# Expert rows loaded behind block 20, and the last three blocks' tokens computed again in slot order

## The reference

```python
h = rmsnorm(x, g_ffn)
g = top1(softmax(h @ w_group))            # one of 4 groups
e_val, e_top = top2(h @ w_er, group g)    # two of its 8 experts
gate = softmax(e_val) * p_top
x = x + sum_j gate[j] * (silu(h @ w_gate[e_j]) * (h @ w_up[e_j])) @ w_down[e_j]
y = rmsnorm(x, g_final)
```

## Time and profile before

| | |
|---|---|
| median of 3 runs | 1202.7 us (1200.88 to 1203.57) |
| the profiled execution's own time | 1198.68 us |
| its span, first to last instruction | 1196.8 us |
| expert blocks, first gathered row to last row out of PSUM | 856.7 to 1149.6 us |
| from there to the end of the span | 47.2 us |

### The profile page before, as it was taken

One profiled execution on the slowest core, in us unless ns is written; L12 is line 12 of the kernel. 1 busy time (PEld: TensorE's weight loads), 2 busy tenths in 40 slices (PEclk: granted clock), 3 DMA queues, 4 the chain that ended last, 5 costly groups with the idle time before them and its releaser, 6 DMA issues.

```text
span 1196.8 us, 19783 instructions
## 1 busy us (share of the span) xinstructions
PE 1097.5 (92%) x7553; PEld 779.2 (65%) x7553; DVE 613.8 (51%) x1631; ACT 480.7 (40%) x1036; POOL 176.5 (15%) x268
## 2 busy tenths in 40 slices
PE   5997799999999899999999899998499999999946
PEld 4984478787878798888989678787243333333312
DVE  6528978888888786723333472365421212121116
ACT  6437678787878524343343451321011111111113
POOL 1320023434342300000000000000102111111002
PEclk8999999999999999999999999999599999999978
DMA  8343140403111134232532635003889999999748
GB/s 285 50 87 64 35 102 1 114 2 84 32 51 40 34 102 123 80 99 62 142 97 80 215 106 220 38 36 129 338 320 393 419 418 418 418 420 417 291 162 340
DMA packets 127253, 205.46 MB, mean 172 GB/s; under 512 B 15108, under 2 KB 100388, under 8 KB 114868
## 3 DMA queue, kind: packets, MB, share of 16 engines
q1 hardware_dynamic: 114868, 177.63, 42.1%
q0 software_dynamic: 10560, 21.02, 5.2%
q10 hardware_dynamic: 1728, 5.51, 1.2%
HBM read 177.85 MB, written 30.18 MB: 174 GB/s over the span
## 4 chain that ended last, share of the span: by engine, by line
PE 76%; DVE 11%; ACT 4%; DMA 4%; issue 3%; POOL 1%; SPq 0%; DVEq 0%; ACTq 0%; POOLq 0%
PE psum L2498 14%; PE psum L2513 7%; PE psum L2213 5%; PE psum L2215 5%; PE psum L2214 5%; DVE place L1464 3%; PE psum L2185 2%; PE psum L2187 2%; PE psum L2186 2%; PE psum L2295 2%; PE psum L2465 2%; PE psum L2364 2%; PE psum L2366 2%; PE psum L2365 2%; PE psum L2269 2%
## 5 line engine op out<-in xcount | busy, mean ns | idle before, releaser
L2498 PE MATMUL psum<-place,place 128*32 128x512 f32 x1536 | 171.1, 597 | 1.2 <-issue 1.2
L1116 ACT ACTIVATE place<-place,place 128x768 uint8<-128x768 f32 (+3 forms) x128 | 125.6, 984 | 6.8 <-DVE place L1495 6.8
L2213 PE MATMUL psum<-place,place 128*128 128x512 f32 x288 | 121.9, 423 | 2.3 <-DVE place L1452 2.3
L2498 PEld LDWEIGHTS psum<-place,place 128*32 128x32 f32 x1536 | 49.0, 110 | 104.8 <-issue 102.3
L2215 PE MATMUL psum<-place,place 128*128 128x512 f32 x288 | 113.4, 394 | 0.0
L2214 PE MATMUL psum<-place,place 128*128 128x512 f32 x288 | 112.6, 391 | 0.0
L1910 DVE TENSOR_TENSOR place<-psum,place 128x256 f32<-128x256 f32 x24 | 10.2, 425 | 156.3 <-ACT place L1296 156.3
L2513 PE MATMUL psum<-place,place 128*32 128x512 f32 x768 | 86.9, 592 | 0.7 <-DVE place L1904 0.7
L2185 PE MATMUL psum<-place,place 128*128 128x256 f32 x288 | 84.9, 295 | 1.6 <-ACT place L1138 1.6
L2186 PE MATMUL psum<-place,place 128*128 128x256 f32 x288 | 81.4, 283 | 0.0
L2187 PE MATMUL psum<-place,place 128*128 128x256 f32 x288 | 81.4, 283 | 0.0
(11 more groups left out here) (323 smaller groups left out, 2428.3 us busy)
## 6 DMA issues: line engine op xcount, KB each, us to landing
place<-in_w_gate SPq DMA_DIRECT2D x32, 1024.0 KB
place<-in_w_up SPq DMA_DIRECT2D x32, 1024.0 KB
place<-in_w_down SPq DMA_DIRECT2D x32, 1024.0 KB
place<-in_w_in SPq DMA_DIRECT2D x28, 512.0 KB, 6.5
place<-expert_out SPq DMA_DIRECT2D x9, 1024.0 KB, 13.0
place<-in_cache_attn_k SPq DMA_DIRECT2D x32, 256.0 KB, 3.3
place<-in_cache_attn_v SPq DMA_DIRECT2D x32, 256.0 KB, 3.4
place<-in_x_prompt SPq DMA_DIRECT2D x3, 1536.0 KB, 8.6
```

The costliest lines, as they stand in the source:

```text
L1116: last = nc.scalar.activation(reached[j], score[j], ACT.Sign, bias=pivot.bitcast(F32)[:, j:j + 1], scale=-1.0, accum_out=minus[:, j - BY_A ...
L2213: nc.tensor.matmul(bank(4 + b), hT_hi[:, k, rows], hi, start=k == 0, stop=False)
L2498: last = nc.tensor.matmul(bank(b % 2)[rows], xT[b % 2][:, k, rows], w_gu[expert_of(b, q) % NSLOT][:, :, k, :], start=k == 0, stop=k == KD - 1)
```

## The change

1. **Loading behind block 20.** SP no longer waits for all 24 blocks. After the scatters of blocks 0 to 20 it loads all nine `y_in` tiles into weight slots that have come free. Blocks 21 to 23 are scattered into a second tensor, `late_rows_out`, and rows of `expert_out` that belong to them stay zero. Both tensors (9.4 MB each) are filled with zeros by SP during the retention heads 0 and 1.
2. **Late blocks in slot order.** For each of the three late blocks POOL gathers the residual rows of its slots (`late_frames`, from a DRAM copy of `x1` that SP now writes before each normed tile), a small table with gates and the other pick's block (`picks_of`, 12 bytes a row) and the row of the other pick (`other_picks`, once from `expert_out`, once from `late_rows_out`). DVE computes the indices (`late_index_all`, 13 small instructions), adds the block's own rows straight from SBUF (`own_pick`) and the others' (`other_pick`). These three are tiles 9 to 11. They are squared, scaled, and scattered by POOL over `y_p` after all eight prompt tiles are stored.
3. **The sample tile** (8) is summed on PE after the late gathers. `ON_PE` is now (5, 6, 7, 8). The final norm runs over 12 tiles instead of 9, in the order `LAST` = 0, 1, 2, 3, 4, 5, 6, 7, 9, 10, 11, 8.
4. **DVE sums some tiles early.** Tiles 0 and 1 stand before `hidden(23)`, tile 2 (behind `late_index_all`) before `rows_out(22)`, tile 3 before `rows_out(23)`.
5. **Overflow.** The overflow blocks and the tables for them move ahead of block 0, inside an `if 0 < n_over` on each engine. All five engines now read `n_over` there, after a short `over_count` on DVE. `over_frames` on PE runs only inside that branch. The loops at the end are gone.

```diff
-ON_PE, LAST_ORDER = (1, 3, 5, 7), (0, 2, 1, 4, 3, 6, 5, 7, 8)
+CUT = NMAIN - 3
+LATE_BLOCKS = range(CUT, NMAIN)
+NLATE = len(LATE_BLOCKS)
+ON_PE = (5, 6, 7, TP)
+BEFORE_HIDDEN, BEFORE_ROWS, BEFORE_LAST = (0, 1), (2,), (3,)
+EARLY_SQUARES = 2
+ON_DVE = tuple(t for t in range(T) if t not in ON_PE)
 STEPS = RH * T
...
+        y_in = [place(at, 2 * D, "p (j d) -> p j d", j=2) for at in (
+            up_at[2], up_at[2] + 2 * D, dn_at[2], up_at[3], up_at[3] + 2 * D, dn_at[3], up_at[4], up_at[4] + 2 * D, dn_at[4])]
+        other_rows = [place(up_at[1] + D * n, D) for n in range(NLATE)]
...
+        LAST = list(ON_DVE) + list(ON_PE[:-1]) + [T + n for n in range(NLATE)] + [TP]
...
+                if h < 2:
+                    sp.wait_ge(pool_set, 4)
+                    empty = late_rows_out if h else expert_out
+                    sp.dma_start(empty.rearrange("(n p) d -> p n d", p=P), zeros.unsqueeze(1).broadcast_to([P, 2 * T, D])).then_inc(zeroed[0], 16)
...
                 sp.wait_ge(h2_done, t + 1)
+                sp.dma_start(x1_dram[t * P:(t + 1) * P, :], x1[:, t, :]).then_inc(x1_out, 16)
                 sp.dma_start(h2_dram[t * P:(t + 1) * P, :], h2[t % 2]).then_inc(h2_out[t % 2], 16)
...
+            sp.wait_ge(*counted)
+            n_over = sp.value_load(over_meta[0:1, NOVER:NOVER + 1], min_val=0, max_val=NOVER)
+            with sp.If(0 < n_over):
...
-            sp.wait_ge(y_out[0], 16 * NMAIN // 2)
-            sp.wait_ge(y_out[1], 16 * NMAIN // 2)
+            sp.wait_ge(y_out[0], 16 * ((CUT + 1) // 2))
+            sp.wait_ge(y_out[1], 16 * (CUT // 2))
             for t in range(T):
+                if t == 3:
+                    sp.wait_ge(gu_ps, last_block(28) + 1)
+                if t == 5:
+                    sp.wait_ge(dn_ps, last_block(28) + 1)
+                if t == 6:
+                    sp.wait_ge(gu_ps, last_block(29) + 1)
+                if t == TP:
+                    sp.wait_ge(dn_ps, last_block(29) + 1)
                 sp.dma_start(y_in[t], expert_out.rearrange("(j t p) d -> t p j d", j=2, p=P)[t]).then_inc(y_loaded(t)[0], 16)
...
+            def late_frames(n):
+                b = CUT + n
+                if n == 2:
+                    pool.wait_ge(h2tr_ps, T + NMAIN)
+                pool.indirect_dma_start(late_x1[n], None, x1_dram, bass.IndirectOffsetOnAxis(ap=block_frames[:, b:b + 1], axis=0),
+                                        bounds_check=NTOK - 1, oob_is_err=False).then_inc(late_x1_in[0], 16)
...
+                pool.indirect_dma_start(late_picks[:, n, :], None, pick_table, bass.IndirectOffsetOnAxis(ap=block_rows[:, b:b + 1], axis=0),
+                                        bounds_check=2 * NTOK - 1, oob_is_err=False).then_inc(late_picks_in[0], 16)
...
+            def other_picks(n, late):
+                pool.indirect_dma_start(other_rows[n], None, late_rows_out if late else expert_out,
+                                        bass.IndirectOffsetOnAxis(ap=late_others[:, late, n:n + 1], axis=0),
+                                        bounds_check=2 * NTOK - 1, oob_is_err=False).then_inc(others_in[0], 16)
...
+            for b in range(2, NMAIN + 5):
+                if b < NMAIN:
+                    gather(b)
+                if b == NMAIN:
+                    pool.wait_ge(*picks_out)
+                    pool.wait_ge(*late_cleared)
+                    pool.wait_ge(x1_out, 16 * RH + 16 * T)
+                    for n in range(NLATE):
+                        picks_of(n)
+                    late_frames(0)
+                    late_frames(1)
+                if b == NMAIN + 3:
+                    for n in range(2, NLATE):
+                        late_frames(n)
+                    pool.wait_ge(*others_ready)
+                    pool.wait_ge(gu_ps, NMAIN)
+                    pool.wait_ge(y_out[0], 16 * ((CUT + 1) // 2))
+                    pool.wait_ge(y_out[1], 16 * (CUT // 2))
+                    for n in range(NLATE):
+                        other_picks(n, 0)
...
+            for x in range(T + NLATE):
+                root(x)
+                if x == 2:
+                    for m in range(2):
+                        pool.wait_ge(y_out[m], 16 * (NMAIN // 2))
+                    pool.wait_ge(others_in[0], 48 + 16 * NLATE)
+                    pool.wait_ge(*y_loaded(TP))
+                    for j in range(2):
+                        pool.indirect_dma_start(y_in[TP][:, j, :], None, late_rows_out, bass.IndirectOffsetOnAxis(ap=sample_late[:, j:j + 1], axis=0),
+                                                bounds_check=2 * NTOK - 1, oob_is_err=False).then_inc(others_in[0], 16)
+                if 2 <= x < 2 + NLATE:
+                    other_picks(x - 2, 1)
+            for m in range(3):
+                pool.wait_ge(y7_out[m], 16 * ((TP + 2 - m) // 3))
+            y_p = o_["y_p"].rearrange("a s d -> (a s) d")
+            for n in range(NLATE):
+                pool.wait_ge(out_done, TP + n + 1)
+                pool.indirect_dma_start(y_p, bass.IndirectOffsetOnAxis(ap=late_write[:, n:n + 1], axis=0), out_rows[T + n], None,
+                                        bounds_check=SEQ - 1, oob_is_err=False).then_inc(late_out[0], 16)
+            pool.wait_ge(*late_out)
...
+            def square(x):
+                t = LAST[x]
+                if t in ON_PE:
+                    act.wait_ge(wo_ps, T + ON_PE.index(t) + 1)
+                    rows = bank(2 * ON_PE.index(t), 0, D)
+                else:
+                    act.wait_ge(*summed(t))
+                    rows = x1[:, t, :] if t < T else late_x1[t - T]
+                if x:
+                    act.wait_ge(ssq_done, 2 * T + x)
...
+            act.wait_ge(gu_ps, NMAIN)
+            for x in range(EARLY_SQUARES):
+                square(x)
             rows_out(NMAIN - 1)
...
+            for x in range(EARLY_SQUARES, T + NLATE + 3):
+                if x < T + NLATE:
+                    square(x)
+                if x >= 3 and LAST[x - 3] < T:
+                    store(x - 3)
...
+            def over_count():
                 L(v, tt(e_cnt, bank(5, 0, NE), C("base"), ALU.subtract))
                 L(v, tt(t_thr, e_cnt.unsqueeze(2).broadcast_to([P, NE, 9]), C("thr").unsqueeze(1).broadcast_to([P, NE, 9]), ALU.is_gt))
                 L(v, nc.vector.reduce_sum(e_blk, t_thr, AX))
                 L(v, nc.vector.tensor_tensor_scan(e_incl, e_blk, e_blk, 0.0, ALU.add, ALU.max))
+                nc.vector.tensor_copy(over_meta[:, NOVER:NOVER + 1], e_incl[:, NE - 1:NE]).then_inc(slots_done, 1)
+                v.wait_ge(*counted)
...
+            def late_index_all():
+                v.wait_ge(*late_picks_in)
+                L(v, ts(late_absent, late_picks[:, :, 2], float(CUT), 2.0 * NTOK, ALU.is_ge, ALU.mult))
+                L(v, tt(late_others[:, 0], late_rows, late_absent, ALU.add))
+                L(v, ts(late_rows, late_rows, 2.0 * NTOK, None, ALU.add))
+                L(v, tt(late_others[:, 1], late_rows, late_absent, ALU.subtract))
+                for n in range(NLATE):
+                    L(v, ts(late_absent[:, n:n + 1], late_picks[:, n, 2:3], float(CUT + n), None, ALU.is_equal))
+                    L(v, ts(late_rows[:, n:n + 1], late_picks[:, n, 2:3], float(CUT + n), 8.0 * NTOK, ALU.is_gt, ALU.mult))
+                L(v, tt(late_second, late_second, late_absent, ALU.mult))
+                L(v, nc.vector.scalar_tensor_tensor(late_frame, late_second, -4.0, late_frame, ALU.mult, ALU.add))
+                tt(late_write, late_frame, late_rows, ALU.add).then_inc(others_ready[0], 1)
...
+            def early_sum(t):
+                v.wait_ge(*y_loaded(t))
+                L(v, nc.vector.scalar_tensor_tensor(x1[:, t, :], y_in[t][:, 0, :], gates[:, 0, t:t + 1], x1[:, t, :], ALU.mult, ALU.add))
+                nc.vector.scalar_tensor_tensor(x1[:, t, :], y_in[t][:, 1, :], gates[:, 1, t:t + 1], x1[:, t, :], ALU.mult, ALU.add).then_inc(x2_done, 1)
+            def own_pick(n):
+                if n == 0:
+                    v.wait_ge(*late_x1_in)
+                    v.wait_ge(y_act, NMAIN)
+                    v.wait_ge(y_dve, NMAIN)
+                nc.vector.scalar_tensor_tensor(late_x1[n], y_of(CUT + n), late_picks[:, n, 0:1], late_x1[n], ALU.mult, ALU.add).then_inc(own_done[0], 1)
+            def other_pick(n):
+                if n == 0:
+                    v.wait_ge(*others_in)
+                v.wait_ge(own_done[0], own_done[1] + n + 1)
+                nc.vector.scalar_tensor_tensor(late_x1[n], other_rows[n], late_picks[:, n, 1:2], late_x1[n], ALU.mult, ALU.add).then_inc(x2_done, 1)
...
+                if b + 1 == NMAIN:
+                    for t in BEFORE_HIDDEN:
+                        early_sum(t)
                 hidden(b)
+                if b + 1 == NMAIN:
+                    late_index_all()
+                    for t in BEFORE_ROWS:
+                        early_sum(t)
                 if b >= 1:
...
+            for t in BEFORE_LAST:
```

(33 more changed lines are left out.)

336 lines of the change are left out of this document (184 added, 152 removed).

## The result

The changed kernel takes 1212.1 us (median of 5 runs, 1209.5 to 1214.6), the kernel before 1202.9 (median of 5, 1200.9 to 1203.6): ratio 1.0083, 95% interval 1.0069 to 1.0097. That is **9.2 us slower**, where I had forecast 5.8 us faster. The profiled execution has a span of 1212.5 us.

What follows compares the result with a forecast made beforehand. The chain that ended last was taken to bound the kernel, 47.9 us behind block 23's last matmul. Front -1.0, last `down` +4.1, then 26.0 and 13.0 end it at 1191.0 instead of 1196.8: -5.8, 1196.9 us, range 1192.0 to 1203.0.

Steps and rivals of the forecast that it cites:

- The front: Everything ahead of the last `down`: -1.0 us (bounds -2.0 and +0.5), with -2.0 from `over_frames` going.
- The 1.0 us for `gate_up(21)`: Two `late_frames` ahead of block 19's scatter delay the weights of `gate_up(21)` on the full DMA: 0 to 2.5, taken 1.0.
- The copies of `x1` add 0.5 MB ahead of each normed tile, 1.2 us on a DMA that is idle there: 0: In the front, residual-row copies ahead of the normed stores were to cost nothing.
- The last `down`: `down(23)` starts 2.8 us later behind DVE's added work and loses 1.3 us to a lower clock, ending at 1153.0.
- From t0 to the last `other_pick`: Serial steps from the end of `down(23)`, t0 = 1153.0, to the last `other_pick` at 1179.0: 26.0 us.
- scatter 23's landing: Behind the last `down`, block 23's scatter lands in 6.2 us, between 4.9 quiet and 8.7 under full DMA.
- the last tile load doesn't come later than scatter 23: The last `y_in` load lands at 1154.5, at most 6.2 us more for scatters and gathers in between.
- the rule that the prediction holds against itself: DVE instructions with two SBUF inputs might hold POOL's five late gathers, by up to 1.3 us each.
- The last landing: Landing of the last late gather, ahead of the last `other_pick`: 5.0 us (4.6 to 8.7).
- DVE's part: Three `other_pick` and the scaling of tile 7, at 1.3 us each, behind the last gather: 5.2 us.
- The end: Square, store of tile 7 and its landing, then POOL's three last scatters and their landing: 13.0 us, to 1192.0.
- Rival D: Slower: four landings in a row at the end take 32.9 instead of 20.1 us; +7.0, 1209.7 us, chance 0.12.

Runs made afterwards that it cites:

- a_end: Changed kernel with the three last scatters ahead of POOL's root of tile 8, and ACT waiting for their landing: 1210.2 us, ratio 1.0070.
- a_tail: `a_end` plus the late gathers of the other picks ahead of the sample's two: 1209.5 us, ratio 1.0059.
- a_best: Changed kernel with all edits that won in a stretch, `late_frames` ahead of scatter 22, sample's gathers behind the eighth root: 1206.7 us, ratio 1.0033.

## Why the prediction was wrong, step by step

**The front** (-1.0 forecast). `over_frames` going was right: 1.9 us for 2.0. The stretch with the tables and branches ahead of block 0, counted at 0, took 0.8 to 2.0 us more than before; no run has them alone, so their share isn't shown. The 1.0 us for `gate_up(21)` wasn't there in this profile: PE was idle for 0.56 us ahead of it, for 1.09 before. The zero fills at 0 were right. The failed step is "The copies of `x1` add 0.5 MB ahead of each normed tile, 1.2 us on a DMA that is idle there: 0". For the first tile the DMA isn't idle: SP had queued 5 MB ahead of it, ACT waited for that store already, and PE for ACT. Measured alone, the copies cost 3.1 us.

**The last `down`** (+4.1) was right in size and cause: 3.8 to 3.9 us, PE idle for 3.68 us, and a `down` of 5.19 instead of 3.64 us. Tile 0's load came 2.5 us after DVE asked for it, mostly because block 20's scatter, which the loads wait for, needed 8.0 us to land where I had 6. That held hidden(23) by 0.8 us; I had tile 1 at 1.5 us early.

**From t0 to the last `other_pick`** (26.0) took 30.8 in the profile after, 1161.6 to 1192.4. Sized wrong: scatter 23's landing (8.5 us for 6.2), and "the last tile load doesn't come later than scatter 23" (it came 1.2 us later; the nine loads took 34.1 us from first issue to last landing, where I had 25.5 and at most 6.2 more). POOL's gathers were right with the hold by DVE, two of five taking 2.08 instead of 1.0 us, so the rule that the prediction holds against itself was right for them and cost 2.1 us, not 5 times 1.3. The last landing (4.9 for 5.0) and DVE's part (5.4 for 5.2) were right.

**The end** (13.0) took 20.1, 1192.4 to 1212.5, and this is the largest miss. The last issue came 0.6 us later than I had it, and that this is close is luck. I had the scatters wait for the store of tile 7; that store landed at 1195.1, 2.7 us behind `other_pick` instead of 5.3. The first scatter came only at 1198.43, behind POOL's last three roots, and in each of them an instruction took about 1 us more beside a wide one of DVE. These are the last two, up to the last root's first instruction:

```profile
1194.11 1.28 POOL L1040 TENSOR_SCALAR place<-place 128x1 f32<-128x1 f32 x1
1195.48 0.55 POOL L1042 TENSOR_TENSOR place<-place,place 128x1 f32<-128x1 f32 x1
1196.11 1.28 POOL L1040 TENSOR_SCALAR place<-place 128x1 f32<-128x1 f32 x1
```

The last scatter landed in 3.4 us, less than my 4.9. The failed step is the sum itself, "Together 13.0": it ends with a landing and has no term for what POOL does after it. What is missing is 7.6 us of drain on POOL and 0.4 around it. I had taken the end of before to be a store's landing. The page shows no row for what ran there, and the chain stops short of the span's end; that gap of 5 us I filled with a landing.

The three misses add up to 3.1 + 4.8 + 7.1 = 15.0 us, which is what lies between -5.8 and +9.2. That they meet so well is luck too, since the first is a difference of medians and the others come from one profile. Within the two profiled executions, 1191.0 forecast and 1212.5 measured, the miss is 21.5 us: 4.8, 7.1, and 9.6 ahead of the end of the last `down` (2.7 at 400 us, 6.1 up to the first gather, 1.6 from there to hidden(0), less 0.8 in the blocks). The other 6.5 us are the choice of executions: the one before was faster than each of the runs in its median, and the one after was the slowest of its five. Rival D named the right side with the wrong mechanism. Its four landings took 8.5, 4.9, 2.6 and 3.4 us, 19.4 together, less than the 20.1 of my sum.

The gain that the change was to bring was there: the last load landed 11 us sooner. It went into 28 us of serial work behind it, into a drain that used to run beside the last store, and into a queue at the front.

## What to carry to other kernels

Work moved under the main loop shortens a kernel only by what is left behind it: count the serial steps behind the last transfer, before and after, on the engine that issues them. A chain of waits that stops short of the span's end is a question to answer first; look at each engine's last instruction, and let the engine with the longest drain finish early. A transfer is hidden only if nothing waits for what stands behind it on its queue.

## What the runs showed of the hardware

- The drain at a program's end took 6.20 us on POOL after an ordinary wait and 7.59 us where it had just issued scatters, whether they had landed or not, and 0.008 us on ACT. In `a_end`, `a_tail` and `a_best` it was over 7.6 us after POOL's last root.
- The idle time of PE that ends at 752 to 757 us and the mean granted clock of 755 to 765 us go together over the seventeen profiles: 2.6 to 2.9 us of idle time with 0.66 to 0.68 (eight), 1.5 to 1.6 us with 0.83 (three), none with 1.00 (five). Only the kernel before had 1.4 us and a clock of 1.00. At 403 to 407 us PE has the same three idle times of 0.9 to 1.0 us in the three profiles whose clock stayed at 1.00 (400 to 410 us) and in eight whose clock fell to 0.83 to 0.88.
- Tiny roots on POOL took 1.28 and 1.47 us instead of 0.19 and 0.55, and issues of gathers 2.08 instead of 1.0, each beside a DVE instruction with two wide inputs in SBUF. Behind 850 us of all seventeen profiles, 37 of the 66 gathers and scatters whose issue overlapped such an instruction by more than 0.3 us took over 1.4 us, and 1 of the 928 others.
